# First mixer of a two-block model: two gate chunks placed between the query chunks, attention scores issued two heads ahead

## What is computed

```
def _mixer(u, w_in, decay_f, decay_b, gn_w, w_ret_out, q_norm_w, w_uq, ...):
    proj = u @ w_in
    rq, rk, rv, rg, a_cq, a_ckv, a_kr, a_gret, a_gmla = jnp.split(proj, SPLIT_IDX, axis=-1)
    ...
    y_ret = _head_group_norm(_bidir_retention(rq, rk, rv, decay_f, decay_b), gn_w)
    y_ret = (jax.nn.silu(rg) * y_ret) @ w_ret_out
    c_q = _rmsnorm(a_cq, q_norm_w)
    q = (c_q @ w_uq).reshape(B, L, MLA_HEADS, MLA_QK)      # a head: 64 plain + 32 rotary columns
    q_nope = q[..., :MLA_NOPE]
    q_rope = _apply_rope(q[..., MLA_NOPE:], mla_cos[:, None, :], mla_sin[:, None, :])
    c_kv = _rmsnorm(a_ckv, kv_norm_w)
    ...
    y_mla = _mla_attention(q_nope, q_rope, k_nope, k_rope, v).reshape(...) @ w_mla_out
    merged = jax.nn.sigmoid(a_gret) * y_ret + jax.nn.sigmoid(a_gmla) * y_mla
    return merged @ w_o
```

## Time and profile before

| | us |
|---|---|
| three timed runs | 1205.74, 1207.40, 1209.52; median 1207.4 |
| the profiled execution: its own time | 1205.34 |
| its span, first to last instruction | 1203.6 |
| PE busy in the span | 1129.1 (94%) |
| DVE busy | 787.3 (65%) |
| ACT busy | 514.3 (43%) |

### The profile page before, as it was taken

How to read it: one execution, slowest core, us unless ns; L and a number is a source line. 1 busy time by engine, 2 the same in 40 slices (tenths; PEclk the granted TensorE clock), 3 DMA queues, 4 the chain that set the end, 5 groups by cost and what they waited for, 6 DMA issues and landing times.

```text
span 1203.6 us, 20984 instructions
## 1 busy us (share of the span) xinstructions
PE 1129.1 (94%) x8618; PEld 1071.2 (89%) x8618; DVE 787.3 (65%) x874; ACT 514.3 (43%) x509; POOL 6.0 (0%) x6
## 2 busy tenths in 40 slices
PE   5999899799899999998986999999988999999998
PEld 4997777588889999988875999999988899999998
DVE  4766778476756666667678565555469787655553
ACT  5323443334444444456275544334254356434331
POOL 0000001000000000000000000000000000000000
PEclk9998999699999999999997999999988999999999
DMA  8743144034435656574521455554443435655630
GB/s 260 229 143 105 40 127 154 1 121 146 140 91 172 186 180 196 170 227 140 164 82 39 137 188 172 199 180 136 138 140 106 142 108 171 210 176 173 209 105 35
DMA packets 160533, 175.70 MB, mean 146 GB/s; under 512 B 4432, under 2 KB 146768, under 8 KB 160352
## 3 DMA queue, kind: packets, MB, share of 16 engines
q1 hardware_dynamic: 160480, 174.95, 46.0%
HBM read 173.89 MB, written 1.05 MB: 145 GB/s over the span
## 4 chain that ended last, share of the span: by engine, by line
PE 75%; DVE 15%; ACT 6%; issue 2%; DMA 0%; SPq 0%; DVEq 0%; ACTq 0%
PE proj L384 47%; PE aux L725 20%; DVE wlo L1304 4%; DVE f L1307 4%; DVE f L1304 2%; PE aux L441 2%; DVE f L1310 1%; ACT whi L967 1%; PE aux L652 1%; PE aux L635 1%; DVE v L1307 1%; DMA f<-in_x_dram 0%; PE aux L645 0%; PE aux L528 0%; PE aux L617 0%
## 5 line engine op out<-in xcount | busy, mean ns | idle before, releaser
L384 PE MATMUL proj<-u,whi 128*128 128x256 f32 (+1 forms) x2912 | 541.4, 287 | 17.0 <-DVE wlo L1304 9.2
L384 PEld LDWEIGHTS proj<-u,whi 128*128 128x128 f32 x2912 | 458.1, 192 | 27.1 <-issue 17.0
L1304 DVE TENSOR_TENSOR wlo<-raw,whi 128x2048 fp32r<-128x2048 f32 (+2 forms) x175 | 374.1, 2137 | 144.5 <-ACT whi L967 137.4
L384 PE MATMUL proj<-u,wlo 128*128 128x256 f32 (+1 forms) x1456 | 414.9, 285 | 0.0
L967 ACT ACTIVATE whi<-raw 128x2048 fp32r<-128x2048 f32 (+2 forms) x175 | 313.5, 1791 | 132.0 <-PE proj L384 76.8
L384 PEld LDWEIGHTS proj<-u,wlo 128*128 128x128 f32 x1456 | 280.4, 193 | 0.0
L725 PE MATMUL aux<-v,whi 128*128 128x256 f32 x1376 | 249.9, 283 | 2.7 <-DVE v L1304 2.5
L725 PEld LDWEIGHTS aux<-v,whi 128*128 128x128 f32 x1376 | 214.2, 192 | 3.4 <-issue 3.4
L725 PE MATMUL aux<-v,wlo 128*128 128x256 f32 x688 | 194.6, 283 | 0.0
L725 PEld LDWEIGHTS aux<-v,wlo 128*128 128x128 f32 x688 | 131.9, 192 | 0.0
L384 PE MATMUL proj<-v,whi 128*128 128x256 f32 (+2 forms) x592 | 111.2, 289 | 9.2 <-DVE v L1304 3.7
(11 more groups left out here) (247 smaller groups left out, 797.2 us busy)
## 6 DMA issues: line engine op xcount, KB each, us to landing
raw<-in_mlp_w_dram SPq DMA_DIRECT2D x64, 1024.0 KB, 5.4
raw<-in_w_in_dram SPq DMA_DIRECT2D x22, 1024.0 KB, 5.3
raw<-in_od_w_in_dram SPq DMA_DIRECT2D x12, 1024.0 KB, 5.3
raw<-in_w_ffn_gate_dram SPq DMA_DIRECT2D x22, 512.0 KB, 4.0
raw<-in_w_ffn_up_dram SPq DMA_DIRECT2D x22, 512.0 KB, 5.2
raw<-in_w_ffn_down_dram SPq DMA_DIRECT2D x21, 512.0 KB, 5.4
raw<-in_ev_w_in_dram SPq DMA_DIRECT2D x10, 1024.0 KB, 5.5
raw<-in_w_ret_out_dram SPq DMA_DIRECT2D x4, 1024.0 KB, 5.2
```

Source lines behind the costliest of these rows:

```text
L384: ins = mm(o, w_of(a, k), x_of(b, k), start=first and k == 0 and j == 0, stop=last and k == kt - 1 and j == 2, skip_group_check=skip)
L1304: return ve.tensor_tensor(o, a, b, op)
```

## The change

The stretch gets another order, and the softmax is rearranged:

- Chunks: `gr0, uq0, gr1, uq1, ukv, gr2, gr3` in place of `uq0, uq1, ukv, gr0..gr3`. PE does `gr0`, the variances, `uq0`, `gr1`, `uq1`. The loop keeps `gr2, gr3, ro0..ro3`: twelve halves, dealt to the heads by `MLA_FILLERS`, so heads 0, 2, 4, 6 have two halves and 1, 3, 5, 7 have one.
- A query chunk of four heads is stored by kind while it is split (4 x 64 plain columns, then 4 x 32 rotary ones), so PE makes two blocks of 128 plain and one of 128 rotary rows: 27 matmuls in place of 36. All rotary rows of a chunk rotate in one matmul, and both chunks in one of 512 columns. The cosine product moves from POOL to DVE, on 2 rows of 256 in place of 8.
- Scores of odd heads go to `proj` banks 2 and 3, those of even heads to `aux` 0 and 1, and are issued two heads ahead; the filler halves use the `proj` bank `order % 2`.
- The scaling of the probabilities moves from DVE to ACT (`mla_scale`).
- `mo0` waits for the four parts of the attention output one by one, the last one only after 36 of its 48 matmuls.

```diff
+MLA_FILLERS = [(0, 1), (2,), (3, 4), (5,), (6, 7), (8,), (9, 10), (11,)]
...
+            project("gr0", t0=META, t=S)
+            pe.wait_ge(sems["d_sq_ready"], 2)
+            for h in range(HEADS):
+                ins = mm(aux[0:8, 0, 0:S], C("pick8")[:, 7 - h:15 - h], d_sq[h // 4][:, h % 4, :], start=h == 0, stop=h == HEADS - 1)
+            ins.then_inc(sems["gn_var"], 1)
             pe.wait_ge(sems["low_done"], 1)
             query_chunk(0)
+            project("gr1", t0=META, t=S)
             query_chunk(1)
...
             kv_half(0)
+            mm(aux[:, 1, :], C("rot_mla"), q_rope, start=True, stop=True).then_inc(sems["q_mla_rotated"], 1)
             kv_half(1)
...
             for h in range(HEADS):
                 mla_turn(h)
-                if h + 1 < HEADS:
-                    mla_scores(h + 1)
-                if h < 4:
-                    project(f"gr{h}", t0=META, t=S, between=lambda: mla_values(h))
...
+                filler(MLA_FILLERS[h][0])
+                mla_values(h)
+                if h + 2 < HEADS:
+                    mla_scores(h + 2)
+                for i in MLA_FILLERS[h][1:]:
+                    filler(i)
...
+            gate(0)
             pump(index["uq0"])
             eng.wait_ge(sems["gn_var"], 1)
             A.post(act(rows8, aux[0:8, 0, 0:S], ACT.Sqrt, bias=gn_eps[0:8], scale=1.0 / P), "gn_root")
+            pump(index["gr1"])
+            gate(1)
+            pump(index["uq1"])
+            pump(index["ukv"])
...
             for h in range(HEADS):
-                name = f"gr{h}" if h < 4 else f"ro{h - 4}"
                 if h + 1 < HEADS:
-                    soft(h + 1)
...
+                    mla_scale(h + 1)
+                for i in MLA_FILLERS[h]:
+                    if i % 2:
+                        pump(index[f"gr{2 + i // 2}" if i < 4 else f"ro{i // 2 - 2}"])
+                        if i < 4:
+                            gate(2 + i // 2)
+                if h + 2 < HEADS:
+                    mla_exp(h + 2)
+                if h in (3, 5, 7):
...
+            gate_part(0)
             for h in range(HEADS):
                 B.run(stt(rg[:, h, :], o_ret[:, h, :], V("gn", h), rg[:, h, :], ALU.mult, ALU.mult))
-            query_part(1)
...
+            query_part(0)
             eng.wait_ge(sems["gn_root"], 1)
             B.post(ve.reciprocal(rows8, rows8), "gn_factor")
+            gate_part(1)
+            query_part(1)
+            kv_part(0)
...
             for h in range(HEADS):
                 eng.wait_ge(sems["prob_turned"], h + 1)
                 B.run(ve.tensor_copy(pt[:, 0:2, :], aux[:, 2, :].rearrange("p (a t) -> p a t", a=2)))
                 B.post(ve.tensor_copy(pt[0:META, 2, :], aux[0:META, 3, 0:S]), "pt_ready")
                 if h + 1 < HEADS:
-                    soft_max(h + 1)
+                    mla_inverse(h + 1)
...
+                if MLA_FILLERS[h][0] % 2:
+                    filler(MLA_FILLERS[h][0])
                 eng.wait_ge(sems["mla_out"], h + 1)
                 p0 = 64 * (h % 2)
                 B.post(ve.tensor_copy(o_mla(h // 2)[p0:p0 + 64, :], aux[p0:p0 + 64, 3, S:2 * S]), "o_mla_ready")
...
+                if h + 2 < HEADS:
+                    mla_max(h + 2)
+                for i in MLA_FILLERS[h][1:]:
+                    if i % 2:
+                        filler(i)
```

More of the change, by code:

```diff
@@ L240, in W, with by_kind, by_head @@
             return t[:, n % RING, off:off + kt * cols].rearrange("p (k n) -> p k n", k=kt)
+        query_chunks = (index["uq0"], index["uq1"])
+        def by_kind(ap):
+            flat = ap.rearrange("p (k n) -> p k n", k=3)
+            return [flat[:, :, a:a + 4 * c].rearrange("p k (h c) -> p k h c", h=4) for a, c in ((0, 64), (256, 32))]
+        def by_head(ap):
+            heads = ap.rearrange("p (k h c) -> p k h c", k=3, h=4)
+            return [heads[:, :, :, 0:64], heads[:, :, :, 64:96]]
         def bc(ap, n):
@@ L248, in build @@
         lgf, lgb = small[:, 4:12], small[:, 12:20]
-        mx, nb, sums, rs = small[:, 20:22], small[:, 22:24], small[:, 24:26], small[:, 26:28]
+        mx, nb, sums, rs = [tuple(small[:, a + 2 * j:a + 2 * j + 2] for a in (20, 32)) for j in range(4)]
         r_tok = small[:, 28:30]
@@ L600, in _ @@
             kv_half(0)
+            mm(aux[:, 1, :], C("rot_mla"), q_rope, start=True, stop=True).then_inc(sems["q_mla_rotated"], 1)
             kv_half(1)
[L603 to L610, removed]
             pe.wait_ge(sems["gn_factor"], 1)
+            pe.wait_ge(sems["q_sin"], 1)
             for h in range(HEADS):
[L614 to L616 removed]
                 ins = mm(aux[:, h // 2, (h % 2) * S:(h % 2 + 1) * S], C("ident")[0:8, h:h + 1].to_broadcast([8, P]), rows8,
@@ L1032, in _, with gate @@
                     A.post(act(t, t, ACT.Tanh, scale=0.5), "gate_tanh")
+            def gate(j):
+                read_out(f"gr{j}")
+                t = yr[:, 2 * j:2 * j + 2, :]
+                A.post(act(t, t, ACT.Tanh, scale=0.5), "gate_tanh")
+            pump(index["gr0"])
+            eng.wait_ge(sems["d_ready"], 1)
+            for e in range(2):
+                A.post(act(d_sq[e], o_ret[:, 4 * e:4 * e + 4, :], ACT.Square), "d_sq_ready")
+            gate(0)
             pump(index["uq0"])
-            pump(index["uq1"])
-            eng.wait_ge(sems["d_ready"], 1)
-            A.post(act(d_sq, o_ret, ACT.Square), "d_sq_ready")
-            pump(index["ukv"])
             eng.wait_ge(sems["gn_var"], 1)
             A.post(act(rows8, aux[0:8, 0, 0:S], ACT.Sqrt, bias=gn_eps[0:8], scale=1.0 / P), "gn_root")
+            pump(index["gr1"])
+            gate(1)
+            pump(index["uq1"])
+            pump(index["ukv"])
             eng.wait_ge(sems["v_turned"], 1)
@@ L1475, in _, with gate_part @@
             B.post(stt(o_ret, auxh, -1.0 / P, o_ret, ALU.mult, ALU.add), "d_ready")
+            def gate_part(j):
+                b = arrive(f"gr{j}")
+                freed(tt(yr[:, 2 * j:2 * j + 2, :], proj[:, b:b + 2, 0:S], bc(rq, 2), ALU.mult))
             def query_part(j):
                 pb = arrive(f"uq{j}")
-                src = proj[0:96, pb:pb + 2, :].rearrange("p a (b t) -> p (a b) t", b=2)
-                freed(tt(q_pre[0:96, 4 * j:4 * j + 4, :], src, bc(r_all[0:96, 1, 0:S], 4), ALU.mult))
+                rkq = r_all[:, 1, 0:S]
+                B.run(tt(q_rope[:, j, :], proj[:, pb + 1, 0:S], rkq, ALU.mult))
+                for e in range(2):
+                    half = slice(64 * e, 64 * e + 64)
+                    src = proj[half, pb, :].rearrange("p (a t) -> p a t", a=2)
+                    ins = tt(q_pairs[0:64, e, 2 * j:2 * j + 2, :], src, bc(rkq[half], 2), ALU.mult)
+                    (freed if e else B.run)(ins)
             def kv_part(half):
```

200 lines of the change are left out of this document (119 added, 81 removed).

## The result

The changed kernel takes 1219.4 us in the median (1216.2 to 1219.9) against 1207.5, 12 us slower by the medians; the ratio is 1.0089 [1.0068, 1.0111], 10.7 us (8 to 13). The forecast had the direction; its 1213.5 is 5.9 us short, and the time lies above its range and above the 1218 behind it. The profiled execution took 1219.66 us, with a span of 1217.9 and a mean granted clock of 0.962 (before: 1205.34, 1203.6 and 0.970).

The account below looks back on a forecast made before the run. TensorE, busy 94% of the span, was taken as the bound, VectorE next. Run-up +12.7 and loop -6.2 gave +6.5 us, from the mean 1207.0 to 1213.5; range 1210 to 1216, with 1207 to 1218 behind it.

Parts of the forecast that it names:

- The gap at `uq1`: Before the first key/value quarter, TensorE stands from 208.8 to 214.85 us until VectorE reads out uq1: 6.0 us.
- The run-up at full clock: Mean sums to head 0's transposes if the clock stays up: transposes at 238.2 us, 10.7 us later than before.
- The waits in the loop: TensorE waits in the attention loop, mostly for VectorE's copy of a head's output: 8.2 us, bounds 0 and 10.
- Head 4's own 1.2: In head 4, transposes' copies come late behind the low part of the attention output: TensorE waits 1.2 us.
- The loop at full clock: Head 0's transposes to `mo0` with the clock up: 59.1 us of work plus 8.2 of waits.
- No wait at `mo0`: At `mo0`, the 1.4 us wait for the attention output goes; its last part is wanted 4.5 us later.
- The half clock: After the gap, the first quarter runs at 2.9 us for 1.6; at the loop's start it costs about 2.4.
- The rival with the clock down from the gap to the loop: Rotation, quarters and spreading also at half clock, run-up about 4 us longer: 1217.5 us; chance 0.10.
- The sign that was missed: Kernel before, 213 to 216 us: clock 0.50 with TensorE busy 1.6 of 3 us, cited against the clock staying up.
- The range: Whole kernel: 1210 to 1216 us; down to 1207 and up to 1218 it leaves out some 2 in 10.
- The loop's saving: Head 0's transposes to `mo0`: 69.7 us where it was 75.9, 6.2 us shorter.
- The table load: ScalarE, before the tanh of `gr1`: 1.28 us without further drain; with the skill's drain the estimate would be 1214.9.

Follow-up runs that it names:

- the kernel in which 4.4 us of it were taken away: Changed kernel with VectorE's splits of gr3 and ro0 moved from ahead of uq1's read-out and the first quarter to behind the last key/value quarter: 1208.0 us, ratio 0.9999.
- the filled kernel: Changed kernel plus 48 idle matmuls before the first key/value quarter and 18, 24, 18 ahead of the transposes of heads 0, 4, 7: 1212.1 us, ratio 1.0033.

## Why the prediction was wrong

The direction was right, and so was the main mechanism, the new gap with the chain of engines that makes it. The step that failed is the term for the half clock. The steps, one by one, measured in the profiled execution from the mean sums on:

- **The gap at `uq1`**: 6.0 forecast, 6.52 measured, by the chain that was forecast; the kernel in which 4.4 us of it were taken away was 11 us faster. Right in place and cause.
- **The run-up at full clock**: 55.1 in the sum with the clock up; 55.7 with the gap and the waits filled. Right, though neither is wholly at the full clock: the sum's 238.2 has the first quarter at half (2.9 us for 1.6), and the filled kernel had the clock low from 225 to 229.
- **The waits in the loop**: 8.2 forecast; 0.34 (ahead of head 3), 2.78, 2.25 and 0.98 (head 6's values) measured, 6.4. Head 4's own 1.2 is absent because its half ran at the low clock, and is there, 1.04, when the waits are filled. The loop at full clock: 67.3 forecast, 67.4 measured. No wait at `mo0`: right.
- **The half clock: the step that failed.** The sum had 2.0 us for it in the run-up (240.2 over 238.2) and 2.4 at the loop's start, 4.4. Measured: 61.15 - 55.66 = 5.5 and 71.66 - 67.36 = 4.3, together 9.8 (7 by the ratios, 3.5 to 10). In the two windows the forecast had 57.1 and 69.7 us, 6.0 less than the 132.8 measured, and 5.4 of these 6.0 are the clock. The profiled execution as a whole was missed by 7.9 (1211.8 forecast, 1219.7 measured); the rest, 0.8 and 1.0, lies before and after the windows, where the sum had nothing. The median was missed by 5.9. The sum let the clock recover after the first quarter, let it drop once more around head 0, and took the loop's waits of 2 to 3 us to cost only their own length. It fell instead a second time in the spreading, and behind heads 4 and 7. The rival with the clock down from the gap to the loop (1217.5) describes the run-up: its 61 us are the 61.15 measured. It had a chance of 0.10 and lacked the falls behind the heads, so that its 1217.5 comes nearest to the 1219.4 is in part luck.
- **The sign that was missed** stands in the kernel before. The sum took the low clock there (0.50 in 213:216, TensorE busy for 1.6 of 3 us) for that of a waiting engine. Finer windows show TensorE busy throughout as the clock fell:

```profile
210.00:213.00 3.00, 3.00 (x15) 1.00 0.00 0
213.00:214.00 1.00, 1.00 (x4) 0.51 0.00 0
```

The work is the spreading, from 210.2 to 214.6; the wait of 1.39 us came only behind it. The 4.37 us that the sum took over for the spreading were partly half clock too: at the full clock it takes 3.69.
- **The range** of 1210 to 1216, and the 1218 behind it, had no room for more low clock than that rival's.
- **The loop's saving** was 4.2 for the 6.2 forecast. The low clock behind heads 4 and 7 cost 4.3 by itself (4.61 + 1.51 and 3.71 + 1.51, for 2.87 + 0.66 each); against it the waits were 1.8 shorter, and head 0's part cost 1.7 (1.54 + 3.71 for the same 3.53), where the sum had 2.4. That is 1.8 of the 2.0.
- **The table load**: it took 1.28 us, and the tanh began 1.30 us after the load did. The Trainium skill ("ScalarE: Activation LUTs", What ACT_TABLE_LOAD costs) has another 1.38 us of drain; this trace does not agree, and the gap is the 6.5 of the rows rather than the 7.4 of that rule.

What stays open is why the clock falls in one execution and not in another with the same order of work. No run here settles it.

## What to carry to other kernels

Work that is moved off a busy stretch must go to where the engine waits for others, not to where the others are already the late ones: two gate chunks put between the query chunks cost 10.5 us, while a version with one of them in head 0's waits, which also loads a table and copies the heads' outputs earlier, is 5 to 7.5 us faster than the kernel before. Where a chunk is split by two engines ahead of its use, look at each engine's queue for a read-out that stands behind a split for something much later: moving two such splits was worth 11 us (7.5 to 14), for a gap that shrank by 4.4. And price a new gap of TensorE with the clock that follows it: here the low clock cost 9.8 us in the profiles and 7 by the ratios, on top of a gap that was forecast to half a microsecond.

## What the runs showed of the hardware

- The granted clock fell with TensorE busy without a pause. In the changed kernel it went from 0.99 to 0.58 between 221 and 227, TensorE busy for 6 of 6 us, with the spreading (weights of 8 rows) as its work from 222 on. The kernel before shows it in the same work (the rows above), and so does the kernel with the gates back in the loop, where the spreading began at 208.46 (length, then busy of PE, PEld, DVE, ACT, POOL, clock, DMA share, GB/s). In the kernel that reads `uq1` out first the same spreading ran at 1.00 throughout, so the work alone does not decide it.

```profile
208.00:211.00 3.00, 2.54 (x10) 2.16 (x11) 2.86 (x5) 0.00 (x0) 0.00 (x0) 0.84 0.17 53
211.00:214.00 3.00, 3.00 (x8) 1.90 (x6) 2.32 (x4) 0.00 (x0) 0.00 (x0) 0.50 0.02 5
```

- It fell behind waits of 2.8 and 2.3 us in the loop, and stayed at 1.00 through waits of 2.1, 2.8, 1.8 and 2.9 us in the run-up of the kernel that reads `uq1` out first; there it fell only after head 0's transposes had begun. Its emptiest stretch of the run-up, TensorE busy for 1.5 of 6 us at 1.00:

```profile
224.00:227.00 3.00, 0.25 (x3) 1.00 0.00 0
227.00:230.00 3.00, 1.26 (x12) 1.00 0.00 0
```

- The times of one program scatter with the clock: the twelve of that kernel run from 1202.2 us at a mean clock of 0.975 to 1212.7 at 0.965. A single profile of such a kernel can be 5 us off its median, so the profiles here carry where the time goes and the ratios how much.
